# Two gaps of 64 bytes between the weight buffers and the features in a two-block transformer kernel

## The chip, the cores and the metric

The kernel runs on one core of one Trainium2 chip. The metric is the device time in microseconds (us), as the median of several runs. Engines are named as in the profile: PE is TensorE (matmuls; PEld its weight loads), DVE is VectorE, ACT is ScalarE, POOL is GpSimd, SP is SyncE, which issues the transfers here. Each engine works through its own instructions in order and waits for others on semaphores. The on-chip memory has 128 partitions; an address in this text is the byte address within a partition, which is the same in all 128.

## The reference

The input is one sequence of 256 tokens with 2048 features, all in float32. Two blocks follow each other.

The first one normalises the embedding and runs two layers. Each layer is `proj = x @ w_in`, three mixers on parts of `proj` (latent attention with 8 heads, pooling over windows, a convolution of width 3), each gated with a silu, then `out = mix @ w_out + b_out` and a layer norm of `ALPHA * x + out`.

The second one is a single layer:

```
x = x + 0.5 * swiglu(rms_norm(x), gate1, up1, down1)        # 2048 -> 5632 -> 2048
x = x + attention_mixers(rms_norm(x)) @ w_out               # 6 + 6 + 4 heads of 128
x = x + 0.5 * swiglu(rms_norm(x), gate2, up2, down2)
```

Nearly all the arithmetic is in products of the 256 tokens with weight matrices, which are read once each.

## The kernel before

**Precision by splitting.** The products must be close to float32 ones, and the kernel makes them from the quicker format `float32r`. Each operand is split into a rounded part (`high`) and the remainder (`low`), and a product is the sum high*high + high*low + low*high. The features are kept with both parts side by side: `xs[:, k, 0:256]` is the rounded part of feature tile k for all tokens, `xs[:, k, 256:512]` its remainder. `hidden`, `mixs`, `lats` and `memh` have the same form.

**The stream of weights.** All weights of both blocks form one sequence of slabs of up to 128 x 2048 elements. A slab passes through three buffers. SyncE loads it into one of four slots of `raw` (L776). ScalarE rounds it into one of two slots of `high` (`split_high`, L1179), in two pieces of up to 1024 elements. VectorE subtracts and writes one of two slots of `low` (`split_low`, L1557), in the same pieces. TensorE waits for `low`, multiplies, and counts `products`, which frees the slots of `high` and `low`. The order of the regions (`in_a`, `uq`, `uk`, `uv`, `in_b`, `out`, `mem`, ..., `up`, `down`) is the list made by `plan()`, and `walk()` takes every engine through it. The regions `up10` to `down20` run as loops over four slabs; small steps of attention, norms and gates are put into slots of the regions by hand (`STEPS`).

**The two forms of a product.** In `product` (L825, L826) the weights are stationary and the features stream. The stationary tile is 128 columns of `high`, the moving one the 512 columns of a feature tile; then 128 columns of `low` with the 256 rounded columns. A tile of 128 output features takes 16 such pairs (11 per half tile in `down`). In `product_natural` (L831 to L833) the features are stationary, 128 tokens at a time, and 512 columns of `high`, `high` and `low` stream. The decay step of one attention has a product of its own: 12 columns of `wfs` stationary, `xs` streaming (L1053). The attention scores and values are plain float32 matmuls (L1100, L1123, L1124).

**Addresses.** `at(name, shape, dt)` gives a buffer the next free address, rounded up to 32 bytes, and moves `cursor` behind it. `raw`, `high`, `low`, `xs`, `x`, `memk`, `memv` and the region `work` (in which `hidden`, `mixs`, `lats` and many others are laid over each other) follow each other in this order. Their sizes are 32, 16, 16, 32, 16, 4, 4 and 62 KB, so before the change all begin at the same address modulo 1024, and the slices of 128 columns at the same address modulo 512. `wfs` comes far behind them; its tiles of 12 columns are 48 bytes apart. An `assert` at the end of the list holds the last address below the memory's usable end.

```
        raw = at("raw", [P, RAW, 16 * P], F32)
        high = at("high", [P, SPLIT, 16 * P], F32R)
        low = at("low", [P, SPLIT, 16 * P], F32R)

        xs = at("xs", [P, KT, 2 * S], F32R)
```

```
            def product(bank_, hi, lo, moving, start, stop):

                eng.matmul(bank_, hi, moving, start=start, stop=False)
                return eng.matmul(bank_[:, S:2 * S], lo, moving[:, 0:S], start=False, stop=stop)
```

Of the kernel before, what the change touches and what calls it, by code (L numbers as in the profile page):

```python
# [309 lines left out]
def build(nc, t):  # L310

    with ExitStack() as ctx:
        cursor = [(nc.sbuf_base + 31) // 32 * 32]

        def at(name, shape, dt, offset=None):
            size = int(np.prod(shape[1:])) * 4
            if offset is None:
                offset = cursor[0]
                cursor[0] += (size + 31) // 32 * 32
            return nc.alloc_sbuf_tensor_at(name, shape, dt, offset=offset)  # L320


        raw = at("raw", [P, RAW, 16 * P], F32)
        high = at("high", [P, SPLIT, 16 * P], F32R)
        low = at("low", [P, SPLIT, 16 * P], F32R)

        xs = at("xs", [P, KT, 2 * S], F32R)
        x_at = cursor[0]
# [1948 lines left out]
```

## Time and profile before

| | us |
|---|---|
| median of 3 runs | 2567.62 |
| the runs | 2566.17, 2567.62, 2578.69 |
| the profiled execution, its own time | 2579.99 |
| its span, first to last instruction | 2578.1 |
| PE busy (14144 matmuls) | 2558.2 |
| DVE busy (2715 instructions) | 1777.7 |
| ACT busy (2105 instructions) | 1355.0 |
| transfers | 480.60 MB, mean 186 GB/s |

The profile is that of one execution, which is one of the longer ones. "Busy" is the time in which an engine had an instruction in flight. Matmuls overlap: each is shown with some 280 to 400 ns, but the next one starts before it ends, so what a matmul costs is the distance from its start to the next one's, and a stretch's cost is read from the number of matmuls that start in it.

### The profile page before, as it was taken

The page shows a single profiled execution, that of the slowest core. Times are in us where ns is not written, and L with a number is a line of the kernel's source. Part 1 is how long each engine was busy: PE and PEld are TensorE (multiplying, and loading weights), DVE is VectorE, ACT ScalarE, POOL GpSimd, SP SyncE. Part 2 cuts the span into 40 slices and gives each one's busy share as a digit, 9 for nine tenths or more (in the row PEclk, how much of TensorE's full clock was granted, in tenths as well). Part 3 has the DMA queues.
Part 4 walks back from the last instruction along what each step waited for, and adds up shares of the span by engine and source line. Part 5 has one row for each costly group of instructions (what it writes and reads, how often), then busy time and mean ns, then how long its engine had stood idle before and what let it go on. Part 6 is the DMA issues. An engine that isn't in the chain of part 4 may idle for free.

```text
span 2578.1 us, 39649 instructions
## 1 busy us (share of the span) xinstructions
PE 2558.2 (99%) x14144; PEld 2212.7 (86%) x14144; DVE 1777.7 (69%) x2715; ACT 1355.0 (53%) x2105; POOL 16.7 (1%) x20
## 2 busy tenths in 40 slices
PE   7999999999999999999999999999999999999999
PEld 6888888888888888888888888888888888888888
DVE  8787668777668666556767766778766655666655
ACT  6665565565566444444444545675544444444443
POOL 2000000000000000000000000000000000000000
PEclk9999999999999999999999999999999999999999
DMA  7554556444554554565555554444554555555454
GB/s 297 197 190 167 202 184 238 168 176 174 205 187 180 187 187 170 192 209 190 185 194 172 182 202 156 155 147 180 182 193 179 181 172 189 204 182 190 165 188 159
DMA packets 75533, 480.60 MB, mean 186 GB/s; under 512 B 8481, under 2 KB 11169, under 8 KB 31137
## 3 DMA queue, kind: packets, MB, share of 16 engines
q1 hardware_dynamic: 75424, 479.16, 52.4%
q8 instruction: 67, 1.10, 0.2%
q14 instruction: 42, 0.34, 0.0%
HBM read 475.72 MB, written 2.10 MB: 185 GB/s over the span
## 4 chain that ended last, share of the span: by engine, by line
PE 83%; DVE 1%; ACT 0%; issue 0%; ACTq 0%; DVEq 0%
PE acc L825 45%; PE acc L826 23%; PE acc L831 3%; PE acc L833 3%; PE acc L832 3%; PE score L825 1%; PE score L1100 1%; PE score L826 1%; PE head_ps L1123 0%; DVE low L1557 0%; PE turn_ps L1109 0%; PE head_ps L1124 0%; PE sums L1043 0%; ACT high L1179 0%; PE sums L1053 0%
## 5 line engine op out<-in xcount | busy, mean ns | idle before, releaser
L825 PE MATMUL acc<-xs,high 128*128 128x512 f32 x3968 | 1395.5, 396 | 2.7 <-DVE mix L1670 1.9
L1557 DVE TENSOR_TENSOR low<-raw,high 128x1024 fp32r<-128x1024 f32 (+2 forms) x972 | 1074.7, 1124 | 444.8 <-ACT high L1179 421.7
L1179 ACT ACTIVATE high<-raw 128x1024 fp32r<-128x1024 f32 (+2 forms) x972 | 942.5, 976 | 486.3 <-PE acc L826 355.3
L826 PE MATMUL acc<-xs,low 128*128 128x256 f32 x3968 | 1111.6, 280 | 0.0
L825 PEld LDWEIGHTS acc<-xs,high 128*128 128x128 f32 x3968 | 745.0, 188 | 178.1 <-DVE mix L1670 2.5
L826 PEld LDWEIGHTS acc<-xs,low 128*128 128x128 f32 x3968 | 750.1, 189 | 0.5
L825 PE MATMUL acc<-hidden,high 128*128 128x512 f32 x1408 | 493.0, 395 | 0.0
L826 PE MATMUL acc<-hidden,low 128*128 128x256 f32 x1408 | 394.8, 280 | 0.0
L1222 ACT ACTIVATE lowsum<-acc 128x256 f32<-128x256 f32 x345 | 131.9, 383 | 498.6 <-PE acc L826 498.2
L825 PEld LDWEIGHTS acc<-hidden,high 128*128 128x128 f32 x1408 | 263.9, 187 | 61.9
L826 PEld LDWEIGHTS acc<-hidden,low 128*128 128x128 f32 x1408 | 266.0, 189 | 0.0
L831 PE MATMUL acc<-high,xs 128*128 128x512 f32 x256 | 105.3, 411 | 0.4 <-DVE scale_a L1621 0.3
L833 PE MATMUL acc<-low,xs 128*128 128x512 f32 x256 | 100.3, 392 | 0.0
L832 PE MATMUL acc<-high,xs 128*128 128x512 f32 x256 | 99.8, 390 | 0.0
L831 PE MATMUL acc<-high,mixs 128*128 128x512 f32 x256 | 99.6, 389 | 0.0
L833 PE MATMUL acc<-low,mixs 128*128 128x512 f32 x256 | 99.6, 389 | 0.0
L832 PE MATMUL acc<-high,mixs 128*128 128x512 f32 x256 | 99.6, 389 | 0.0
L1233 ACT ACTIVATE silu_g<-gate 128x256 f32<-128x256 f32 x86 | 36.0, 418 | 91.4 <-DVE gate L1632 91.4
L1631 DVE TENSOR_TENSOR up<-acc,lowsum 128x256 f32<-128x256 f32 x86 | 36.5, 424 | 68.6 <-ACT lowsum L1222 68.4
L825 PE MATMUL acc<-mixs,high 128*128 128x512 f32 x224 | 79.2, 399 | 0.0
L826 PE MATMUL acc<-mixs,low 128*128 128x256 f32 x224 | 62.9, 281 | 0.0
L1631 DVE TENSOR_TENSOR gate<-acc,lowsum 128x256 f32<-128x256 f32 x86 | 36.5, 424 | 35.6 <-ACT lowsum L1222 35.3
(387 smaller groups left out, 2026.2 us busy)
## 6 DMA issues: line engine op xcount, KB each, us to landing
raw<-w_up_dram SPq DMA_DIRECT2D x176, 1024.0 KB, 4.8
raw<-w_down_dram SPq DMA_DIRECT2D x128, 704.0 KB, 4.0
raw<-w_in_dram SPq DMA_DIRECT2D x76, 1024.0 KB, 4.8
raw<-w_out_dram SPq DMA_DIRECT2D x32, 1024.0 KB, 4.8
raw<-w_heads_dram SPq DMA_DIRECT2D x24, 1024.0 KB, 4.8
raw<-w_mixout_dram SPq DMA_DIRECT2D x16, 1024.0 KB, 4.8
raw<-w_mem_dram SPq DMA_DIRECT2D x8, 1024.0 KB, 4.7
raw<-w_nat_dram SPq DMA_DIRECT2D x8, 1024.0 KB, 4.8
```

The lines of the kernel that those rows point to most:

```text
L825: eng.matmul(bank_, hi, moving, start=start, stop=False)
L826: return eng.matmul(bank_[:, S:2 * S], lo, moving[:, 0:S], start=False, stop=stop)
L831: eng.matmul(bank_, xh, hi, start=start, stop=False)
L832: eng.matmul(bank_, xl, hi, start=False, stop=False)
L833: return eng.matmul(bank_, xh, lo, start=False, stop=stop)
L1100: last = eng.matmul(score[n % 2][:, b, 0:w], qc[:, b * P:(b + 1) * P], kc[:, 0:w], start=(m == 0), stop=(m == len(qk) - 1))
L1179: eng.activation(high[:, s % SPLIT, to:to + n * P], raw[:, s % RAW, at_:at_ + n * P], ACT.Copy).then_inc((highs_a, highs_b)[piece], 1)
L1222: eng.activation(lowsum_of(r, T), acc_of(r, T)[:, S:2 * S], ACT.Copy, scale=0.5 if r.kind == "down" else 1.0).then_inc(low_ready, 1)
L1233: eng.activation(silu_g[:, :], gate[:, :], ACT.Silu).then_inc(silu_done, 1)
L1557: eng.tensor_tensor(low[:, s % SPLIT, w], raw[:, s % RAW, at_:at_ + n * P], high[:, s % SPLIT, w].bitcast(F32), ALU.subtract).then_inc((lo ...
L1631: step_(eng.tensor_tensor(out_[:, :], first, second, ALU.add))
```

## The change

`cursor` is moved on by 64 bytes behind `high` and again behind `low`. `raw` and `high` stay where they are, `low` begins 64 bytes later, and everything that is allocated behind it 128 bytes later. Nothing else is changed.

```diff
         raw = at("raw", [P, RAW, 16 * P], F32)
         high = at("high", [P, SPLIT, 16 * P], F32R)
+        cursor[0] += 64
         low = at("low", [P, SPLIT, 16 * P], F32R)
+        cursor[0] += 64
 
         xs = at("xs", [P, KT, 2 * S], F32R)
         x_at = cursor[0]
```

## Rows read from the trace of the kernel before

**Rows 1.** The page: busy engines, clock by slice, chain of the end by line.

```profile
PE 2558.2 (99%) x14144; PEld 2212.7 (86%) x14144; DVE 1777.7 (69%) x2715; ACT 1355.0 (53%) x2105; POOL 16.7 (1%) x20
...
PEclk9999999999999999999999999999999999999999
...
PE acc L825 45%; PE acc L826 23%; PE acc L831 3%; PE acc L833 3%; PE acc L832 3%; PE score L825 1%; PE score L1100 1%; PE score L826 1%; PE head_ps L1123 0%; DVE low L1557 0%; PE turn_ps L1109 0%; PE head_ps L1124 0%; PE sums L1043 0%; ACT 
```

**Rows 2.** Waits: who waited for whom, total us, times, longest us.

```profile
PE score L1155 <- DVE z L2037: 13.2, 1, 13.2
...
ACT lowsum L1222 <- PE acc L826: 498.2, 318, 4.4
```

**Rows 3.** Windows of PE: from:to, us, PE busy (matmuls), clock, DMA share, GB/s.

```profile
960.00:1080.00 120.00, 120.00 (x694) 1.00 0.52 178
...
1800.00:1920.00 120.00, 120.00 (x681) 1.00 0.51 185
```

**Rows 4.** Timeline from 1234 us: start, duration, engine, line, operation, out<-in, forms, count.

```profile
1234.15 0.39 PE L825 MATMUL acc<-xs,high 128*128 128x512 f32 x1
...
1234.70 2.10 ACT L1179 ACTIVATE high<-raw 128x1024 fp32r<-128x1024 f32 x2
...
1234.84 0.39 PE L825 MATMUL acc<-xs,high 128*128 128x512 f32 x1
...
1235.54 0.39 PE L825 MATMUL acc<-xs,high 128*128 128x512 f32 x1
...
1235.85 2.36 DVE L1557 TENSOR_TENSOR low<-raw,high 128x1024 fp32r<-128x1024 f32 x2 [1.58 <-ACT high L1179]
...
1236.92 0.39 PE L825 MATMUL acc<-xs,high 128*128 128x512 f32 x1
...
1238.31 0.39 PE L825 MATMUL acc<-xs,high 128*128 128x512 f32 x1
```

**Rows 5.** Timeline from 2299 us, first and last of ten L825 starts.

```profile
2299.66 0.40 PE L825 MATMUL acc<-xs,high 128*128 128x512 f32 x1
...
2302.84 0.40 PE L825 MATMUL acc<-xs,high 128*128 128x512 f32 x1
```

**Rows 6.** Windows of the matmuls of L825 alone, one for each pair.

```profile
0.00:780.00 780.00, 488.22 (x1376) 1.00 0.55 198
780.00:1527.00 747.00, 732.33 (x2112) 1.00 0.54 189
...
1740.00:2578.20 838.20, 832.12 (x2355) 1.00 0.52 182
...
460.00:520.00 60.00, 56.04 (x159) 1.00 0.49 167
```

**Rows 7.** Windows of the matmuls of L831 alone, the whole span.

```profile
0.00:2578.20 2578.20, 236.76 (x592) 1.00 0.53 186
```

**Rows 8.** Timeline from 1528 us: the twelve-column products, then the natural form.

```profile
1528.43 3.87 PE L1053 MATMUL sums<-xs,wfs 128*12 128x512 f32 x16
...
1532.14 0.40 PE L831 MATMUL acc<-high,xs 128*128 128x512 f32 x1
...
1533.52 0.39 PE L831 MATMUL acc<-high,xs 128*128 128x512 f32 x1
...
1534.65 0.39 PE L833 MATMUL acc<-low,xs 128*128 128x512 f32 x1
```

**Rows 9.** Lines by form: count, busy us, mean ns, idle before.

```profile
L1557 DVE TENSOR_TENSOR low<-raw,high 128x1024 fp32r<-128x1024 f32 x696 | 835.2, 1223 | 288.5 <-ACT high L1179 267.2 <-DVE hidden L1639 16.6
...
L1179 ACT ACTIVATE high<-raw 128x1024 fp32r<-128x1024 f32 x696 | 729.0, 1055 | 294.3 <-PE acc L826 164.3 <-PE acc L833 122.4 <-PE score L826 3.0
```

**Rows 10.** DMA issues: out<-in, queue, count, KB each, us to landing.

```profile
raw<-w_up_dram SPq DMA_DIRECT2D x176, 1024.0 KB, 4.8
```

**Rows 11.** Timeline from 1742 us: plain float32 matmuls of an attention.

```profile
1742.27 0.60 PE L1123 MATMUL head_ps<-turned,v_nat 128*128 128x256 f32 x2
1742.71 0.38 PE L1124 MATMUL head_ps<-turned,v_nat 128*128 128x128 f32 x2
```

## The prediction

> **What bounds the kernel now.** I read the page first: TensorE's matmuls are busy for 2558.2 of 2578.1 us, VectorE for 69%, ScalarE for 53%, at a granted clock of 9 tenths or more in every slice; 68% of the chain that ended last lies on two TensorE lines of one helper, L825 and L826 [rows 1]. Then the waits. The longest one that TensorE has is 13.2 us, once, at the start; the long totals are all of ScalarE and VectorE waiting for TensorE or for each other [rows 2]. So there is no stall to remove. What is left to ask is how far apart the matmuls start, because the spacing is the time. (A "busy" matmul says nothing on this: its span overlaps the next one.)
>
> **The spacing.** In windows of equal length I counted matmuls. The 120 us from 960 us on hold 694 of them; the 120 us from 1800 us on hold 681 [rows 3]. That is 172.9 against 176.2 ns each, or 346 against 352 ns for a pair (one of 512 columns on the rounded weights, one of 256 on the remainders). The timeline gives it closer. In the first stretch 12 pairs take 1238.31 - 1234.15 = 4.16 us, 346.7 ns each [rows 4]. In the second, 9 pairs take 2302.84 - 2299.66 = 3.18 us, 353.3 ns each [rows 5]. I call these the **short** and the **long pace**. The granted clock is 1.00 in both [rows 3], which is the 2.4 GHz level; 768 columns at one a cycle would need 320 ns. So a pair carries 26.7 ns beyond its columns at the short pace and 33.3 ns at the long one, and the difference, 6.6 ns, is the time of 16 columns, or 64 bytes of a partition. This is the only thing in the profile that a shift by 64 bytes could act on. By line, 2112 pairs start between 780 and 1527 us, 2355 between 1740 us and the end, and 1376 before 780 us [rows 6]: 5857 in all. The other order of operands (L831 to L833) has three times 592 matmuls of 512 columns [rows 7], which follow each other at 0.226 us: 1533.52 to 1534.65 us holds five [rows 8].
>
> **The change, part by part.** No instruction, wait, loop or transfer is added, removed or moved on any queue. What changes is numbers in operands. Before, every large buffer has a size that is a multiple of 512 bytes and follows the one before without a gap, so `high`, `low`, `xs`, `hidden`, `mixs` and `lats` all begin at the same place modulo 512, and so does each 128-column slice of them. After, `low` lies 64 bytes further and everything behind it 128 bytes further. Of a pair, then, the stationary tile of L825 lies 128 bytes off its moving tile, that of L826 64 bytes off.
>
> *Other engines.* Do writes and reads of ScalarE and VectorE now collide with TensorE's reads, so that a shift would relieve it? The short stretch has a ScalarE split from 1234.70 us on for 2.10 us, and a VectorE pair of splits from 1235.85 us for 2.36 us. The two pairs from 1234.84 us, beside ScalarE alone, take 0.70 us; the four from 1236.92 us, where VectorE alone splits, take 1.39 us [rows 4]: 350 and 347.5 ns, equal within the rows' 10 ns. Cost and gain: 0. Could the splits themselves change? They take 1223 and about 1055 ns for 1024 elements, with 288.5 and 294.3 us idle before them [rows 9]. A tile of 16 pairs takes 16 x 0.347 = 5.6 us and needs two splits on each engine, 2.4 us of VectorE. VectorE's total reserve is 2578 - 1778 = 800 us [rows 1] against 835.2 us for all of its full-sized splits [rows 9], so these would have to take nearly twice as long before they set the pace. Bounds from 0 to no effect: 0 us.
>
> *Transfers.* `raw` is not moved, and it takes nearly all bytes. A load lands after 4.8 us [rows 10] in a ring of four slots, each of which is due every 22 us. Other transfers land 128 bytes further. 0 us.
>
> *TensorE's own reads.* Here no row isolates the effect, so I bound it from both sides. The nearest rows are those of L1053: its 16 stationary tiles are 12 columns wide and 48 bytes apart, so their starts run through four places modulo 64 and every one of those modulo 128 that 16-byte steps allow, while the moving tiles are `xs` as elsewhere. They take 1532.14 - 1528.43 = 3.71 us, 232 ns each, as against 226 ns where both tiles are aligned alike [rows 8]. Tiles at other low addresses are thus not quicker; if anything they are 6 ns slower. Secondly, both paces occur with the same buffers at the same addresses: the loops of the first feed-forward part hold the short one (2112 pairs in 732.33 us, 346.8 ns each) and those of the second the long one (2355 in 832.12 us, 353.3 ns) [rows 6]. The pace is not a function of the address alone; it looks like the relative timing with which a stretch is entered and which it then keeps. I take 0 for this term, the value of the nearest rows, and keep both ends: all pairs at the short pace, which saves 2355 x 6.6 ns = 15.5 us and, if about half of the first 1376 are long (56.04 us for 159 of them between 460 and 520 us is 352 ns [rows 6]), some 4 us more; and all pairs at the long pace, which adds 2112 x 6.6 ns = 13.9 us and the same 5 us.
>
> **The sum.** The profiled execution took 2579.99 us: a span of 2578.1 and 1.9 us around it. Changes: 0. The median of the runs shown is 2567.62 us, 12.4 us lower, and their highest is 2578.69. The end "all short" of the profiled execution is 2580.0 - 15.5 - 4 = 2560.5 us, so I read the median as an execution in which most of the last stretch went at the short pace; this is an inference. Nothing in the change says that this mix moves, so I forecast the median again, **2568 us**, with 2561 to 2580 as its own range.
>
> **A rule beside this.** The rows show no wait of TensorE for another engine's access to memory [rows 2, 4]. The Trainium skill, SBUF — State Buffer, "Who interferes with whom", speaks against the change in the same sense: matmul operand and weight load have a read port each, TensorE shares neither, and never waits on anyone. By that rule the sum is unchanged, at 2568 us; that two paces exist at all is not foreseen there.
>
> **Rivals.**
> *Faster: the equal low addresses cost every matmul something now.* For it: 26.7 ns per pair beyond the columns, and the plain f32 matmuls, which ask for a moving element half as often, come near their column time: two instructions of 256 columns on L1123 take 1742.71 - 1742.27 = 0.44 us, 220 ns each, where 512 column times are 213 [rows 11], and their tiles are aligned alike too. Against it: L1053 at other addresses is not quicker [rows 8]. If each of the 2 x 5857 + 1776 = 13490 matmuls lost its whole 13.3 ns, 180 us would go, and the long pace with it: 2580 - 180 - 19 = 2381 us. If the collision is one step of 6.7 ns for each, 90 us: 2471 us. The place is every weight load beside a moving stream; it decides from the first pair on.
> Beside it stands a figure of the Trainium skill, TensorE: Matmul & The Clock Gate, "Wait — 56ns, not 53.3ns?": bf16 matmuls in a stream start N / 2.4 GHz + about 2.5 ns apart, some 216 ns for 512 columns. By that figure, an estimate, a pair would take 325 ns and the kernel about 2410 us; no row here comes to it with these operands.
> *Slower: 64 bytes bring the load of `low` into step with the moving stream.* The load of the remainders' tile runs beside the 512-column matmul. If the step by 64 bytes is just the one by which the long pace is longer, then every stretch could fall into it, also the 2112 pairs that now hold the short pace [rows 4, 6]: 2580 + 13.9 + 5 = 2599 us. For it: the size of the step, and that L1053's mean lies above the aligned case [rows 8]. Against it: the same addresses give either pace now. It decides where the first feed-forward part is entered, at 780 us.
> *The change has no reach where it matters.* All starts stay multiples of 64 bytes apart and each tile is 512 contiguous bytes or more, so both streams still go through all places modulo 512. Then only the timing at the entries decides, and the time is the forecast's. It is counted with the forecast.
>
> **How the numbers follow.** The measurement of this kernel can tell some 0.5% from no change, here 12.8 us: 2554.8 to 2580.5 us is "same". Forecast, with all its mixes of the paces: 0.68. Faster rival: 0.14. Slower rival: 0.16, plus 0.02 for a mix that by chance ends just above 2580.5. The range goes from 2560 us (all short) to 2600 us (all long): it holds the forecast and the slower rival, 0.86 together, and gives up the faster one.
>
> **What would show it.** Right: in equal windows of the profile after, counts of about 694 or 681 matmuls per 120 us and nothing else, pairs of 346.7 or 353.3 ns, L1053 at 3.7 us for 16, VectorE's splits at 1223 ns. The faster rival would show as counts above 694, at 740 for full relief. The slower one as 681 everywhere, between 960 and 1320 us too. What would make me wrong: a spacing that is neither, or a spacing that changes only where `low` is loaded.

## The result

The changed kernel takes 2585.16 us in the median of 20 runs, the kernel before 2566.18 us in the median of 20. The ratio of all runs is 1.0059, with a 95% interval of 1.0042 to 1.0075 (that of the two medians alone is 1.0074): slower, by about the 0.5% that the prediction took as the least that can be told. The forecast was 2568 us; the time lies in the stated range of 2560 to 2600 us, but outside the 2561 to 2580 us given for the likeliest case.

The medians hide how the times lie. They form levels:

```
                  level 1            level 2            level 3
before, 20 runs   16: 2563.8-2567.7   4: 2578.7-2582.0   0
after, 20 runs     4: 2569.5-2570.3  13: 2583.6-2586.1   3: 2598.5-2599.3
```

Two things have moved. The two levels that both kernels reached lie 4 and 5 us later, and the executions lie mostly on the second level instead of the first. How often before takes which level differs between series of runs: it was on the first in 15 of 15 runs of a later series, in 7 of 11 of another, and in 5 of 11 of a third, where three lay on a third level at 2594.3 to 2595.0 us. In the series in which all 15 were on the first level, the one execution of the changed kernel took 2585.5 us, its second. So the shift of the shares is likely the change's, but its size is not settled.

The profiled execution of the changed kernel is one of the first level: it took 2569.63 us. The page (busy us and share, number of instructions):

```profile
span 2567.7 us, 39649 instructions
...
PE 2545.8 (99%) x14144; PEld 2211.2 (86%) x14144; DVE 1777.9 (69%) x2715; ACT 1354.9 (53%) x2105; POOL 17.2 (1%) x20
```

The instructions are the same ones, and VectorE and ScalarE are busy as long as before, within 0.2 us [rows 1]. The largest group of splits, which had a mean of 1223 ns [rows 9]:

```profile
L1559 DVE TENSOR_TENSOR low<-raw,high 128x1024 fp32r<-128x1024 f32 x696 | 835.6, 1224 | 291.1 <-ACT high L1181 270.5 <-DVE hidden L1641 16.6
```

So the other engines are as predicted, and what differs is TensorE's spacing. (Lines are two further down: L827 here is L825 of before.) First all matmuls in two windows of 120 us, then the pairs alone in three stretches (us of the window, PE busy, matmuls that start in it):

```profile
960.00:1080.00 120.00, 120.00 (x695) 1.00 0.52 181
1800.00:1920.00 120.00, 120.00 (x695) 1.00 0.54 188
...
0.00:780.00 780.00, 485.95 (x1376) 1.00 0.55 197
780.00:1527.00 747.00, 732.33 (x2112) 1.00 0.54 189
1740.00:2600.00 860.00, 821.21 (x2368) 1.00 0.51 178
```

Both stretches hold the short pace, where in the profiled execution of before the second had 681 matmuls in its window [rows 3] and 832.12 us for 2355 pairs [rows 6]. That is why this profile is shorter than before's although the kernel is slower: the two profiles come from different levels. What is dearer shows in the natural form. The first matmul of a group of three, and that of the third group after it:

```profile
300.21 0.39 PE L833 MATMUL acc<-high,mixs 128*128 128x512 f32 x1
...
302.29 0.39 PE L833 MATMUL acc<-high,mixs 128*128 128x512 f32 x1
```

Nine matmuls in 2.08 us are 231 ns each; before they were 226 ns apart [rows 8].

### The profile page after: what moved, and what is told of

The parts are those of the page before. It is cut to its first block, busy times and chain, and to the rows that moved or that the text cites. A ratio compares the mean times of both kernels' runs of the same rounds, so it can differ in the third digit from the quotient of the medians.

```text
span 2567.7 us, 39649 instructions
## 1 busy us (share of the span) xinstructions
PE 2545.8 (99%) x14144; PEld 2211.2 (86%) x14144; DVE 1777.9 (69%) x2715; ACT 1354.9 (53%) x2105; POOL 17.2 (1%) x20
## 4 chain that ended last, share of the span: by engine, by line
PE 97%; DVE 2%; ACT 1%; issue 0%; DMA 0%; ACTq 0%; DVEq 0%
PE acc L827 50%; PE acc L828 26%; PE acc L833 5%; PE acc L835 5%; PE acc L834 5%; PE score L827 2%; PE score L1102 1%; PE score L828 1%; PE head_ps L1125 1%; DVE low L1559 0%; PE turn_ps L1111 0%; PE head_ps L1126 0%; ACT high L1181 0%; DVE scale_a L1852 0%; DVE lat L1855 0%
## 5 line engine op out<-in xcount | busy, mean ns | idle before, releaser
L827 PE MATMUL acc<-xs,high 128*128 128x512 f32 x3968 | 1384.5, 393 | 4.9 <-DVE xs L2079 2.7
L827 PEld LDWEIGHTS acc<-xs,high 128*128 128x128 f32 x3968 | 745.0, 188 | 170.3 <-DVE xs L2079 3.4
L827 PE MATMUL acc<-hidden,high 128*128 128x512 f32 x1408 | 488.3, 392 | 0.0
L827 PEld LDWEIGHTS acc<-hidden,high 128*128 128x128 f32 x1408 | 264.2, 188 | 57.8
L827 PE MATMUL acc<-mixs,high 128*128 128x512 f32 x224 | 77.7, 392 | 0.0
L833 PEld LDWEIGHTS acc<-high,xs 128*128 128x128 f32 x256 | 48.1, 188 | 12.4 <-issue 2.2
```

Of the source, the lines that this page charges most:

```text
L833: eng.matmul(bank_, xh, hi, start=start, stop=False)
```

## The experiments

Two theories stood against each other. **Theory A**: the distances between the buffers have a price of their own in the spacing of the matmuls. **Theory B**: only the timing at which a stretch is entered counts, and the change shifted that by accident.

### The same kernel at the second level

No edit: the changed kernel again, to catch an execution of another level.

> The changed kernel once more, to see an execution at a level above the lowest. Theory A with entries: a time near 2585 us comes from one of the two feed-forward stretches at 353.3 ns a pair and the other at 346.7, with all else as in the first profile (natural form 231.1 ns). A rival: the 15.6 us are spread over the whole span.

It took 2585.5 us, and its windows, in the same order as above, are:

```profile
960.00:1080.00 120.00, 120.00 (x695) 1.00 0.53 181
1800.00:1920.00 120.00, 120.00 (x681) 1.00 0.52 184
...
0.00:780.00 780.00, 485.48 (x1376) 1.00 0.55 197
780.00:1527.00 747.00, 732.33 (x2112) 1.00 0.54 189
1740.00:2600.00 860.00, 837.20 (x2368) 1.00 0.51 178
```

The last stretch has the long pace, 837.20 - 821.21 = 16.0 us more for the same 2368 pairs, and nothing else has changed. The two executions are 15.9 us apart. So the second level is the first one with the last feed-forward stretch at the long pace, and a stretch keeps its pace for hundreds of microseconds. The third level would then be the first stretch at the long pace too (2112 pairs at 6.6 ns, 13.9 us; the levels lie 13.7 us apart); it was not profiled.

The two traces also show where the executions part. Behind the plain float32 matmuls of an attention, TensorE starts a run of pairs without having waited; the first pair takes some 430 ns in both, the twelve from the second one on 4.16 us in one and 4.24 us in the other. First the execution of the first level, then that of the second:

```profile
1748.16 0.47 PE L827 MATMUL score<-mixs,high 128*128 128x512 f32 x1
...
1748.60 0.39 PE L827 MATMUL score<-mixs,high 128*128 128x512 f32 x1
...
1752.76 0.39 PE L827 MATMUL score<-mixs,high 128*128 128x512 f32 x1
```

```profile
1748.47 0.48 PE L827 MATMUL score<-mixs,high 128*128 128x512 f32 x1
...
1748.89 0.40 PE L827 MATMUL score<-mixs,high 128*128 128x512 f32 x1
...
1753.13 0.40 PE L827 MATMUL score<-mixs,high 128*128 128x512 f32 x1
```

That is 346.7 against 353.3 ns, from the second pair on, at the same addresses.

### All buffers 64 bytes later

```diff
+        cursor[0] += 64
         raw = at("raw", [P, RAW, 16 * P], F32)
```

> 64 bytes left free ahead of all buffers, so that all lie 64 bytes later and their distances are those of before the change. Only distances count: times on the levels of before, 2565 and 2580 us, natural form 226.7 ns. The absolute address counts: another level, as after the whole change or beyond.

The median is 2567.82 us, the ratio 1.0003 (0.9994 to 1.0012), and all 11 runs lie between 2566.3 and 2568.9 us. Its profile is also one of before's distances at the first level, and both stretches are short there (694 matmuls in the second window too, where the profiled execution of before had 681):

```profile
1800.00:1920.00 120.00, 120.00 (x694) 1.00 0.53 189
```

A shift of everything by 64 bytes does not count; what the change does, it does through the distances between the buffers.

### One gap without the other

Behind the rounded weights alone:

```diff
         high = at("high", [P, SPLIT, 16 * P], F32R)
+        cursor[0] += 64
         low = at("low", [P, SPLIT, 16 * P], F32R)
```

> The gap behind the rounded weights alone: remainders and features both 64 bytes off the rounded weights. Theory A: the natural form (1776 matmuls) costs about 231 instead of 226.7 ns, 8 us in all, as after the whole change, and the times lie on levels near 2570, 2585 and 2599 us, according to which of the two feed-forward stretches holds the long pace. Theory B: levels near 2565 and 2580 us as before the change, natural form at 226.7 ns.

Behind the remainders alone:

```diff
         low = at("low", [P, SPLIT, 16 * P], F32R)
+        cursor[0] += 64
 
         xs = at("xs", [P, KT, 2 * S], F32R)
```

> The gap behind the remainders alone: both weight buffers where they were, all features 64 bytes off both. Theory A: as with the other gap alone, the natural form at about 231 ns and levels near 2570, 2585, 2599 us; if only the distance between rounded weights and remainders matters, levels of before, 2565 and 2580 us, with the natural form at 226.7 ns. Theory B: levels and natural form as before the change.

Neither theory had this. With the gap behind the rounded weights the kernel takes **2538.99 us**, ratio 0.988 (0.9854 to 0.9906), and six runs lie within 2.4 us. With the gap behind the remainders it takes **2608.07 us**, ratio 1.0147 (1.012 to 1.0174), and six runs lie within 1.1 us. The two halves of the change pull in opposite directions, and no run of either lies a level apart from the others. The windows of the gap behind the rounded weights (all matmuls, then pairs):

```profile
960.00:1080.00 120.00, 120.00 (x708) 1.00 0.53 182
1800.00:1920.00 120.00, 120.00 (x708) 1.00 0.53 189
...
0.00:780.00 780.00, 479.04 (x1376) 1.00 0.55 198
780.00:1527.00 747.00, 718.28 (x2112) 1.00 0.55 192
```

and of the gap behind the remainders:

```profile
960.00:1080.00 120.00, 120.00 (x681) 1.00 0.52 178
1800.00:1920.00 120.00, 120.00 (x682) 1.00 0.52 185
...
0.00:780.00 780.00, 493.47 (x1376) 1.00 0.54 196
780.00:1527.00 747.00, 732.21 (x2072) 1.00 0.53 184
```

718.28 us for 2112 pairs are 340.1 ns each, a third pace that no stretch of before had; 732.21 us for 2072 pairs are 353.4 ns, the long pace in both stretches. The natural form costs more in both cases. With the gap behind the rounded weights nine matmuls take 302.27 - 300.16 = 2.11 us, 234 ns each:

```profile
300.16 0.39 PE L832 MATMUL acc<-high,mixs 128*128 128x512 f32 x1
...
302.27 0.40 PE L832 MATMUL acc<-high,mixs 128*128 128x512 f32 x1
```

The sum for the quicker one, from before's first level (2566 us, both stretches short): the pairs from 780 us on lose 732.33 - 718.28 = 14.1 us in the first stretch and 6.6 ns x 2368 = 15.6 us in the second, those before 780 us some 5 to 9 us [rows 6], and 1776 natural matmuls gain 8 ns each, 14 us. That gives 2566 - 14.1 - 15.6 - 7 + 14 = 2543 us, against 2539 measured. Summed in the traces from each start to the next one's, and set against the shift of everything (first level, before's distances), the pairs before 780 us take 9.9 us less (490.7 to 480.8) and the natural matmuls only 10.5 us more; with these the sum is 2537 us, and the waits of TensorE for `xs`, 0.7 us there and 2.4 us here, add most of the rest.

### The distances by themselves

What the distances cost was then measured without the model. The kernel leaves out all of the reference's computation: it copies `x` into buffers and runs short stretches of the two forms, each after a pause, with the tiles' starts moved by slicing. Its core:

```
for k, (kind, (h, l, x), count, _) in enumerate(segs):     # h, l, x: bytes / 4
    eng.wait_ge(go, k + 1)
    for b in range(count):
        if kind == "pair":
            eng.matmul(a, high[:, h + b * P:h + (b + 1) * P], xs[:, x + 512 * b:x + 512 * b + 512], ...)
            eng.matmul(a[:, S:2 * S], low[:, l + b * P:l + (b + 1) * P], xs[:, x + 512 * b:x + 512 * b + S], ...)
```

I write a place as (high, low, features) in bytes: before is (0, 0, 0), the change (0, 64, 128), the first gap alone (0, 64, 64), the second alone (0, 0, 64).

> A kernel that leaves the whole model out and runs only short stretches of matmuls, each after a pause: 16 pairs of the form of L825 and L826, or 24 matmuls of the form of L831 to L833, with the stationary and the moving tiles at 14 choices of low addresses, four entries each. Theory A (the relation of the low addresses has a price of its own): with all tiles at equal places the natural form starts every 226.7 ns, with the weights at 0 and 64 and the features at 128 bytes every 231.1 ns, whatever the entry; for the pairs some choices should give 346.7 and some 353.3 ns at all four entries. Theory B (only the timing at the entry counts): the spacings differ between entries, in the same way for every choice, and all choices have the same mean within 1 ns.

The pairs at (0, 0, 0), at two entries, and at (0, 64, 64); each couple of rows spans the eleven or twelve pairs at the end of a stretch (L89 is the 512-column matmul):

```profile
34.19 0.40 PE L89 MATMUL acc<-xs,high 128*128 128x512 f32 x1
...
38.08 0.40 PE L89 MATMUL acc<-xs,high 128*128 128x512 f32 x1
...
40.28 0.39 PE L89 MATMUL acc<-xs,high 128*128 128x512 f32 x1
...
44.09 0.40 PE L89 MATMUL acc<-xs,high 128*128 128x512 f32 x1
...
112.97 0.39 PE L89 MATMUL acc<-xs,high 128*128 128x512 f32 x1
...
117.05 0.39 PE L89 MATMUL acc<-xs,high 128*128 128x512 f32 x1
```

3.89 us for 11 pairs are 353.6 ns; 3.81 us for 11 are 346.4 ns, at the same addresses; 4.08 us for 12 are 340.0 ns. The three paces of the whole kernel are all here, with no other engine at work beside TensorE. The natural form at (0, 0, 0), (0, 64, 128) and (0, 64, 64), six groups of three each:

```profile
399.24 0.40 PE L98 MATMUL acc<-high,xs 128*128 128x512 f32 x1
...
403.33 0.39 PE L98 MATMUL acc<-high,xs 128*128 128x512 f32 x1
...
411.20 0.40 PE L98 MATMUL acc<-high,xs 128*128 128x512 f32 x1
...
415.36 0.39 PE L98 MATMUL acc<-high,xs 128*128 128x512 f32 x1
...
435.48 0.40 PE L98 MATMUL acc<-high,xs 128*128 128x512 f32 x1
...
439.70 0.40 PE L98 MATMUL acc<-high,xs 128*128 128x512 f32 x1
```

4.09, 4.16 and 4.22 us, or 227, 231 and 234 ns a matmul, just as in the whole kernels. At (0, 256, 0) pairs and natural form had the values of (0, 0, 0), at (64, 64, 64), where all lie 64 bytes later, too. The remainders alone moved, (0, 64, 0), gave 346.7 ns at all four entries, and (0, 0, 16) gave 346.7 ns at two entries and 360.0 at two, the longest of all. Of twelve-column tiles, 21 matmuls with the tile at one aligned place, and 21 with tiles 48 bytes apart:

```profile
725.86 5.03 PE L105 MATMUL acc<-xs,high 128*12 128x512 f32 x21
...
749.81 5.03 PE L105 MATMUL acc<-xs,high 128*12 128x512 f32 x21
```

The same 5.03 us: for such tiles the place makes no difference. This bears on the prediction, below. Theory A is right in that distances have a price of their own, theory B in that at some distances the pace differs from entry to entry; neither was right alone.

The same kernel with 8 x 8 places:

> Again a kernel that leaves the model out: pairs and natural products in short stretches, now with the remainders and the features at each of 8 x 8 distances of 0 to 224 bytes, in steps of 32, behind the rounded weights. Theory A (distances modulo 256 set the spacing): the pair has its minimum, 340 ns, at remainders +64 and features +64, and no other place below it by more than 2 ns; the natural form has its minimum, 680 ns for three, only where the features lie level with the weights, and 693 to 704 elsewhere. A rival: the minimum is reached wherever the two streams that run at the same time lie 64 bytes apart in the right direction, so the map is a function of one difference for each of the two matmuls.

Mean ns of a pair at three entries, worked out from the starts in the trace. Rows: remainders behind the rounded weights; columns: features behind the rounded weights, both in bytes.

```
            0            32           64           96           128          160          192          224
  0    347/347/353  347/347/347  349/353/353  350/350/350  351/351/351  347/347/347  353/353/353  353/347/352
 32    347/346/346  347/347/353  349/349/349  353/353/352  351/351/351  351/351/351  353/353/352  351/349/349
 64    347/347/347  349/349/349  340/340/350  347/347/347  347/353/347  352/353/353  351/351/351  347/347/350
 96    347/347/352  346/346/347  348/347/347  349/350/350  347/347/347  353/353/353  348/348/353  354/353/353
128    350/347/347  347/347/347  347/353/347  347/347/350  352/352/353  350/349/350  353/353/353  351/351/351
160    347/351/347  349/349/349  349/349/349  349/349/349  351/351/350  347/347/350  351/351/351  350/351/351
192    351/347/350  353/353/353  353/347/347  353/354/354  353/347/347  352/352/343  340/350/340  347/350/346
224    354/354/354  352/352/352  350/349/350  347/347/347  351/351/352  354/347/347  351/351/351  350/351/351
```

Mean ns of three natural matmuls at two entries, the places that matter here:

```
            0        64       128      192
  0      680/682  700/700  698/698  688/688
 64      695/696  703/701  694/693  697/695
128      700/693  693/693  686/687  691/691
192      688/688  686/695  697/697  699/699
```

A pair has its minimum, 340 ns, at (64, 64), and once more at (192, 192). The natural form has it at (0, 0) alone, but 686 to 688 ns at several other places, which the expectation did not have. The change moves between two places of these maps: from (0, 0) to (64, 128) a pair gains nothing and the natural form loses 13 ns in three. The rival fails on the map. Where remainders and features lie equally far behind the rounded weights, the stream and the tile loaded beside it are level in the 512-column matmul, and yet the pair's best value runs from 340 to 352 ns; and a sum of two functions, one of each matmul's difference, fitted to the 64 mean values, explains 28% of their variance.

Whether the pause before a stretch chooses its pace:

> The model left out again: stretches of 14 pairs at four choices of distances, each after pauses of 48 lengths that differ by one VectorE element (about 1 ns) each. If the pace is chosen by the timing at the entry, then before's distances (0, 0, 0) show 346.7 and 353.3 ns both, in an order that follows the pause, and the changed kernel's (0, 64, 128) show both too, with the long one more often (its last stretch was long in 16 of 20 runs, before's in 4 of 20). The gap behind the rounded weights alone (0, 64, 64) shows 340 or 350 ns, and the gap behind the remainders alone (0, 0, 64) mostly 353 ns. If the entry doesn't matter, each choice has one value.

```
48 pauses, stretches of 14 pairs, rounded ns of a pair : how many
(0, 0, 0)      353: 40   347: 8
(0, 64, 128)   353: 2    347-348: 46
(0, 64, 64)    350: 19   340-342: 29
(0, 0, 64)     352-353: 35   349: 13
```

Each choice has more than one value at the same addresses, and a stretch holds its value to the end, so the value is set at the entry. But it follows no order in the length of the pause, and the shares are the reverse of what I expected: the changed kernel's distances show the long pace less often here than before's, while in the whole model the changed kernel has it more often. A stretch in the model is entered from other matmuls (above, from plain float32 ones, without a wait), not after a pause. That a pace is set at the entry is shown; what at the entry sets it is **open**, since no pause was repeated and no matmuls of another form stood ahead of a stretch here.

### Each form at its best place

The map says that pairs and natural form want different distances. In this kernel a slot of `low` lies 64 bytes behind `high` for pairs and level with it for the natural regions; `xs`, `hidden` and the `mixs` of the second block lie at 64, the `mixs` of the output projections and `memh` at 0. Small buffers fill the gaps.

```diff
-        low = at("low", [P, SPLIT, 16 * P], F32R)
+        low_at = cursor[0]
+        for_pairs = [at(f"low_p{n}", [P, 16 * P], F32R, low_at + 64 + n * 8448) for n in range(SPLIT)]
+        for_natural = [at(f"low_n{n}", [P, 16 * P], F32R, low_at + n * 8448) for n in range(SPLIT)]
...
-        mixs = at("mixs", [P, KT, 2 * S], F32R, work)
+        mixs_to = [at(f"mixs{n}", [P, KT, 2 * S], F32R, work - 64 * (n < DEPTH)) for n in range(DEPTH + 1)]
...
+                if i is None and s >= 2 and piece == 0 and r.kind != "natural" and region_of(s - 2).kind == "natural":
+                    eng.wait_ge(products, released(s - 2, 1))
```

> Each form at its best place of the map: for all pairs remainders and features 64 bytes behind the rounded weights (340 ns a pair), for the natural products of the two output projections and of the memory both level with them (680 ns for three), for the other natural products remainders level and features at 64 bytes (700 ns). Theory A: 960 natural matmuls fall from 234.1 to 226.7 ns against the gap behind the rounded weights alone, 7.1 us, the other 768 by half a microsecond in all: about 2531 us, in one level. A rival: the extra wait where a slot goes from a natural to a pair slab, or the new addresses of small buffers, take the gain back: 2536 us or more.

> The gap behind the rounded weights alone once more, on the same chip as the kernel with both forms placed: 2539 us within 1 us in every run, if its pace doesn't depend on how a stretch is entered; a second level near 2560 us or higher, if it was luck.

On one chip the two took 2534.69 us (six runs, 2533.9 to 2535.3) and 2539.42 us (six runs, 2538.5 to 2541.4). The ratios to before are 0.9828 (0.9779 to 0.9876) and 0.9846 (0.9798 to 0.9895); they flatter the change, and their intervals are wide, because before's own eleven runs there were spread over all three levels, 2565 to 2595 us. Against before's first level, 2566 us, the quicker one is 1.2% faster; whether either is 2% faster than before as it runs, the intervals leave open. The gain over the first gap alone is 4.7 us of the 7 to 8 expected, and the time lies between the 2531 us of theory A and the 2536 of its rival. The natural form came down as it should, here nine matmuls in 2.04 us, 227 ns each:

```profile
300.26 0.39 PE L840 MATMUL acc<-high,mixs 128*128 128x512 f32 x1
...
302.30 0.39 PE L840 MATMUL acc<-high,mixs 128*128 128x512 f32 x1
```

and the added wait took part of it back. Waits of TensorE (total us, times, longest):

```profile
PE score L1164 <- DVE z L2048: 13.0, 1, 13.0
PE acc L834 <- DVE low_p L1568: 3.0, 2, 1.5
```

The second row is not among those of the first gap alone. It is the rival's mechanism at 3.0 us. Summed from start to start, and without the two waits, the natural matmuls take 7.1 us less than with the first gap alone, just as expected; the waits took some 3 us back. The version is the quickest one here, and the gap behind the rounded weights alone is the cheap way to most of it.

The repeat of the first gap alone missed what was expected of it in two of its six runs: they took 2541.4 us, some 2 us more than the other four. One of the two is the profiled one, and its trace shows where that lies: some 250 pairs 10 ns dearer each, 2.5 us. From 1735 to 1823 us the pairs come every 350 ns, where the earlier profile of the same kernel has 340; then two matmuls of 256 columns stand between two pairs (L1138 and L1139, of a norm), and behind them the pairs come every 340 ns, with no wait of TensorE in between. Twenty-four pairs from 1760.20 us, and 24 from 1827.88 us:

```profile
1760.20 0.40 PE L826 MATMUL acc<-mixs,high 128*128 128x512 f32 x1
...
1768.60 0.40 PE L826 MATMUL acc<-mixs,high 128*128 128x512 f32 x1
...
1827.88 0.39 PE L826 MATMUL acc<-xs,high 128*128 128x512 f32 x1
...
1836.04 0.39 PE L826 MATMUL acc<-xs,high 128*128 128x512 f32 x1
```

So this placement too has a second pace, 350 ns as in the short stretches; it was left at the first matmuls of another form, while the feed-forward loops held 340 ns.

## Why the prediction came out as it did

**Right: what bounds the kernel, and that the spacing is what could move.** VectorE's and ScalarE's busy times did not change; TensorE's longest wait stayed at 13.1 us. Its waits for `xs` took 2.7 us instead of 0.6, but that is not the placement's: they are 2.4 us in one profile of the first gap alone and 0.7 us in the other.

**Right: the two paces, their step and what they are worth.** The 16.0 us between two executions of the changed kernel is the term "2355 x 6.6 ns = 15.5 us" of the sum, and 13.7 us between its upper levels the term of 13.9. The reading of before's median as an execution with the last stretch at the short pace fits its levels and the profile of the shift of everything. The signs named for being right all came: windows of 695 or 681 matmuls, pairs of 346.7 or 353.3 ns, 3.69 us for the twelve-column products, splits of 1224 ns. They were blind to what else moved, since none of them looked at the natural form. (One count is short of its parts: 2112, 2355 and 1376 pairs make 5843; the other 14 of the 5857 lie between 1527 and 1740 us.)

**Luck: that the time lies in the range.** The likeliest case had 2568 us and at most 2580; 2585 us is inside because the range was stretched to the slower rival's 2599. Three runs of 20 met that end, but not by its sum: the 5 us that it has for the pairs before 780 us did not come (487.1 us from start to start, as against 489.1 before), and the natural form, which it has at nothing, added 5.6 us.

**Wrong: "I take 0 for this term".** Two things were hidden in it. First, the natural form had a price of its own: 231 instead of 226 ns in the rows shown. Summed from start to start over the whole traces its matmuls take 5.6 us more than before. Against the shift of everything, an execution of before's distances at the same level, the pairs before 780 us take 3.6 us less (490.7 to 487.1) and the waits for `xs` are 2.0 us longer: 5.6 - 3.6 + 2.0 = 4.0 us, which is the distance of the first levels (2569.9 - 2565.9). Second, the mix of the paces moved: of before's 20 runs 4 lie above the first level, of the changed kernel's 16. That is the larger part of the 19 us between the medians, and why these distances fall into the long pace more often in the whole kernel is open. The sentence "nothing in the change says that this mix moves" was an absence of knowledge, used as if it were evidence. That both paces occur at equal addresses shows that something other than the address takes part; it doesn't show that the address takes none.

**Wrong: the nearest row.** The term's value came from L1053, whose tiles lie at all kinds of places and which is not quicker. In the stretches without the model, twelve-column tiles take the same at one aligned place as at places 48 bytes apart, and in the changed kernel L1055, as it is there, has

```profile
1532.40 3.85 PE L1055 MATMUL sums<-xs,wfs 128*12 128x512 f32 x16
1536.09 0.39 PE L833 MATMUL acc<-high,xs 128*128 128x512 f32 x1
```

3.69 us for 16, as against 3.71 [rows 8]. The row is blind to the address, so it could not bear on the question. It was near in its form and in the line of the code, not in the thing that was asked of it; its 232 ns do not come from its addresses.

**The rivals.** The slower one had the right effect for the run's mix (more stretches at the long pace) but its reason is not enough. It names 64 bytes between the remainders' tile and the moving one. Both the whole change and the second gap alone have them, and in the short stretches (0, 64, 128) holds the short pace 46 times of 48, (0, 0, 64) the long one 35 times: how far the features lie behind the rounded weights counts as well. The gap between rounded weights and the rest makes the kernel quicker, and the gap behind the remainders costs. The change undoes with its second gap what its first one gains: 2539 with the first, 2608 with the second, 2585 with both. The faster one was right in that distances cost something now, and the first gap alone recovers 27 us of it; its price of one step of 6.7 ns is the one found for a pair, 347 to 340 ns, not for each matmul. For the natural form equal low addresses are the best place on the map, against this rival, and the full relief of 180 us exists nowhere on it.

**The rule.** The Trainium skill, SBUF — State Buffer, "Who interferes with whom", gives matmul and weight load a read port each and has TensorE never wait. By it all these kernels would take the same. The stretches with TensorE alone at work differ by 4% in a pair (340 to 354 ns, and 360 at one place) with the distance between its own tiles and the entry, so here the measurement decides against it; that no other engine takes part, the trace bears out.

## What to carry to other kernels

When one engine sets the time without waiting, look at the spacing of its instructions to the nanosecond, and compare it across stretches: two values for one form are a sign of something that can be tuned. Test the distance between the operands' buffers one gap at a time, and at small steps, since two changes that each matter can cancel; a kernel with TensorE alone maps them all in one run. Such a map tells which paces a placement has, but not how often a whole kernel will hold each. And take many runs before and after, in one series: here a median of three can fall on any of the levels, 14 to 16 us apart, while a placement whose runs all lie within 3 us is worth something by itself.

## What the runs showed of the hardware that was not expected

- The spacing of float32r matmuls depends on the distances between the buffers of stationary and moving tiles: 340 to 354 ns for a pair of 512 and 256 columns in steps of 32 bytes (360 ns at one entry in two with the features 16 bytes off), 680 to 707 ns for three of 512. An offset of 256 gave the values of 0, and moving everything together changed nothing (2567.82 against 2566.89 us).
- At some distances two paces are possible at the same addresses, 346.7 and 353.3 ns, and a stretch keeps the one it was entered with for 700 us and more. In whole kernels the pace was set, or changed, behind matmuls of another form, without a wait of TensorE.
- At (0, 64, 64) a pair takes 340 ns, 20 ns above its 768 columns at 2.4 GHz. 350 ns was seen there too: in short stretches (19 of 48), and for 88 us of one profile of the whole kernel; the feed-forward loops held 340 ns.
- What makes these steps is open. The paces 340, 346.7, 350, 353.3 and 360 ns lie multiples of 3.3 ns apart, 8 columns at 2.4 GHz; the values of 349, 351 and 352 ns on the map do not.
